# A hybrid decoder layer on one core: three activation blocks requested ahead of the big weight quarters, and the last root applied as a factor per partition

## The chip, the cores and the metric

The kernel runs on one core of one Trainium2 chip. The metric is the device time of one execution in microseconds (us), lower is better. Rows of the profile call the engines PE (TensorE), DVE (VectorE), ACT (ScalarE), POOL (GpSimd) and SP (SyncE, which here issues every transfer between memory and the on-chip buffers).

## The reference

One layer over 1024 tokens of width 1024, all in float32:

```
mod = silu(c) @ w_ada + b_ada            # nine rows: shift, scale, gate, three times
u = rmsnorm(h, ffn1_norm)*(1+sc1)+sh1;   h = h + 0.5*gt1*swiglu(u, ffn1_w_in, ffn1_w_out)
u = rmsnorm(h, mix_norm)*(1+sc2)+sh2;    h = h + gt2*token_mixer(u)
u = rmsnorm(h, ffn2_norm)*(1+sc3)+sh3;   h = h + 0.5*gt3*swiglu(u, ffn2_w_in, ffn2_w_out)
out = rmsnorm(h, final_norm)             # x * rsqrt(mean(x*x) + eps) * gain
swiglu(x, w_in, w_out) = (silu(g) * v) @ w_out,  g, v = split(x @ w_in)     # hidden width 2816
```

The token mixer (gated linear attention and differential attention) is not touched by the change.

## The kernel before

The activations `h` are kept transposed: 128 channels on the partitions, 8 channel tiles `k`, 1024 tokens along the row. Tokens are worked in two halves of 512. Each float32 operand of a product is split into a high part and a low part, and a product is three matmuls (high by high, high by low, low by high). ScalarE makes the high part, GpSimd the low part of a weight and VectorE the low part of an activation.

**The down projection of each FFN** (`down(f)`, f = 0 and 1) is done with seven products of half-size blocks in place of eight. Each product goes over the 11 pairs of hidden tiles, so there are 77 steps `n` of 12 matmuls (line 2428). A step needs one activation block, 128x512, from `hid_dram`: the hidden activations are written to memory block by block (`hidden_out`, 256 KB each) and read back (`hidden_in(f, n)`, 256 KB) into four buffers `x_raw`, by turns. ScalarE copies block n to its high part (`x_highs`, line 1251), VectorE subtracts for the low part (`x_low`, line 1818, which counts up `x_ready`). `hidden_in(f, n)` with n >= 4 waits until `x_ready` says that block n - 4 has been split. `x_op`, the split operand, has three buffers, so ScalarE can take block n when step n - 3 has been done.

The weights come in four quarters, Q00, Q10, Q01 and Q11, each 11 blocks of 256 KB. Q00 comes in parts: loads 6 and 0 (2 and 6 blocks), 1 (2 blocks) and 2 (the last block); loads 3, 4 and 5 are Q10, Q01 and Q11 whole, 2816 KB each. Products 0, 1 and 6 use Q00, Q01 and Q11 as they are; the others use sums (`weight_sum`, half of them on GpSimd, half on VectorE): Q00 - Q10 from step 4 on, then Q11 less that, from step 15 on, and so on. ScalarE makes the high part of the weight of step n + 3 in its turn n, right behind the activation block n (`high_hs`), so from turn 8 on it needs Q01.

SyncE issues all loads and stores in one written order, and waits where that order says so. The waits on `hs_used` are for products of the last hidden tile, whose operands lie where the quarters go. The wait on `hid_out` is for all stores of activations, before the first block that the last hidden tile has written is read (product 1 on).

**The tail.** Product 6 gives the channel tiles 4 to 7 of the second token half, into the banks `ps[4]` to `ps[7]`. VectorE adds them to `h` (`reads(1, 6)`, line 1873), ScalarE squares them (line 1152), VectorE adds the squares up over the channel tiles (line 1726), TensorE sums over the partitions with a matrix of ones (`mean_square`, line 2261), ScalarE takes the root (lines 1157 and 1160), VectorE multiplies `h` by gain and root (`final_y`, line 1731), TensorE transposes 128x128 pieces (line 2807), four to a bank, ScalarE copies each bank into `o_tile` (line 1617), and SyncE stores one tile of 128 tokens by 1024 channels (512 KB) at a time. The first token half has its root and its scaling during the last steps of the down projection; its transposes come right behind the last step.

## Time and profile before

| | |
|---|---|
| median of 3 runs | 2260.81 us (2259.23 to 2266.37) |
| the profiled execution | 2263.8 us, span 2262.1 us from the first to the last instruction |
| mean granted TensorE clock | 0.987 of full speed |
| TensorE busy | 2181.8 us, 96% of the span |
| VectorE, ScalarE, GpSimd busy | 1266.0, 817.0, 1286.4 us |
| moved by DMA | 236.27 MB, 104 GB/s over the span |

The span is what the profile covers; the execution's own time is 1.7 us more. Shares are of the span. The granted clock is 1.00 at 2.4 GHz and 0.50 at 1.2 GHz. The down projection of the first FFN runs from about 501 to 710 us, that of the second from 2017 to 2237 us.

### The profile page before, as it was taken

The numbers are of one execution on the slowest core, as the hardware profiler recorded it, in microseconds if no ns is written. First come the engines' busy times: TensorE is split into PE (matmuls) and PEld (weight loads), VectorE is DVE, ScalarE is ACT, GpSimd is POOL, SyncE is SP. The second block draws the span as 40 slices with busy tenths as digits, with TensorE's granted clock in tenths as the row PEclk, the third lists the DMA queues.
The fourth block names the chain that finished last, engine by engine and source line by source line (L and its number), as shares of the span: only waits on it lengthen the run. The fifth ranks groups of instructions, "written<-read, shape, count | busy, mean of one in ns | idle before, by whom it ended". The sixth has DMA issues, their size and how long they took to land.

```text
span 2262.1 us, 27922 instructions
## 1 busy us (share of the span) xinstructions
PE 2181.8 (96%) x10289; PEld 1761.5 (78%) x10289; DVE 1266.0 (56%) x1971; ACT 817.0 (36%) x1513; POOL 1286.4 (57%) x1036
## 2 busy tenths in 40 slices
PE   7999999998999999999999999999999999999997
PEld 4688888886887777778777788888778888878886
DVE  6956666667857327656655202243955444458845
ACT  5522232233445314355545201023523333233444
POOL 5677878878854432312212233336778887768841
PEclk9999999999999999999999999999999999999999
DMA  9054454566333310011101113111053333364332
GB/s 345 28 168 154 152 159 139 169 233 215 94 102 113 103 47 1 11 29 38 29 28 31 45 47 121 47 47 47 24 174 115 112 98 112 98 257 147 99 98 103
DMA packets 222793, 236.27 MB, mean 104 GB/s; under 512 B 9775, under 2 KB 154306, under 8 KB 222402
## 3 DMA queue, kind: packets, MB, share of 16 engines
q1 hardware_dynamic: 222658, 234.49, 31.9%
q8 instruction: 83, 1.36, 0.2%
q14 instruction: 52, 0.43, 0.1%
HBM read 185.69 MB, written 48.76 MB: 104 GB/s over the span
## 4 chain that ended last, share of the span: by engine, by line
PE 77%; DVE 8%; ACT 4%; DMA 3%; issue 3%; POOL 2%; SPq 1%; DVEq 0%; ACTq 0%; POOLq 0%
PE ps L2371 30%; PE ps L2428 15%; PE ps L2242 13%; PE ps L2325 12%; POOL w_lo L987 1%; DMA x_raw<-hid_dram 1%; DVE h L2038 1%; DMA ada_full<-in_w_ada 1%; PE ps L2513 1%; PE ps L2623 1%; PE ps L2287 1%; DVE x_op L1818 1%; ACT h L1485 1%; PE ps L2588 1%; DVE h L2061 1%
## 5 line engine op out<-in xcount | busy, mean ns | idle before, releaser
L2428 PE MATMUL ps<-x_op,w_hi 128*128 128x512 f32 x1232 | 385.0, 394 | 13.5 <-DVE x_op L1818 13.5
L2371 PE MATMUL ps<-t,w_hi 128*128 128x512 f32 x1280 | 395.5, 390 | 1.1 <-POOL w_lo L987 1.0
L987 POOL TENSOR_TENSOR w_lo<-w_raw,w_hi 128x512 fp32r<-128x512 f32 x240 | 347.4, 1460 | 63.1 <-ACT w_hi L1241 63.1
L952 POOL TENSOR_SCALAR w_hi<-w_raw 128x1024 fp32r<-128x1024 f32 x55 | 57.8, 1050 | 471.3 <-PE ps L2242 295.7
L1241 ACT ACTIVATE w_hi<-w_raw 128x512 fp32r<-128x512 f32 x240 | 143.8, 626 | 414.7 <-DMA w_raw<-in_ffn_w_in 172.7
L2428 PEld LDWEIGHTS ps<-x_op,w_hi 128*128 128x128 f32 x1232 | 233.5, 190 | 65.1 <-issue 14.5
L2371 PEld LDWEIGHTS ps<-t,w_hi 128*128 128x128 f32 x1280 | 239.4, 188 | 52.3 <-POOL w_lo L987 2.4
L987 POOL TENSOR_TENSOR w_lo<-q,w_hi 128x512 fp32r<-128x512 f32 x132 | 193.2, 1468 | 125.4 <-ACT w_hi L1241 125.4
L2371 PE MATMUL ps<-t,w_lo 128*128 128x512 f32 x640 | 249.1, 389 | 0.0
L2428 PE MATMUL ps<-x_op,w_lo 128*128 128x512 f32 x616 | 241.6, 392 | 0.0
L1818 DVE TENSOR_TENSOR x_op<-x_raw,x_op 128x512 fp32r<-128x512 f32 x154 | 161.8, 1062 | 120.4 <-ACT x_op L1251 119.8
L2371 PE MATMUL ps<-b_low,w_hi 128*128 128x512 f32 x640 | 197.3, 389 | 0.9 <-POOL w_lo L987 0.9
L1251 ACT ACTIVATE x_op<-x_raw 128x512 fp32r<-128x512 f32 x154 | 97.3, 632 | 238.4 <-PE ps L2428 205.3
L958 POOL TENSOR_TENSOR w_lo<-w_raw,w_hi 128x512 fp32r<-128x512 f32 x128 | 178.1, 1411 | 7.0 <-ACT w_hi L1283 1.8
L1648 DVE SCALAR_TENSOR_TENSOR ada_acc<-ada_half,c_act,ada_acc 128x512 f32<-128x512 f32 x84 | 95.2, 1134 | 141.4 <-DMA ada_half<-in_w_ada 141.4
L2242 PE MATMUL ps<-u_hi,w_hi 128*128 128x512 f32 x368 | 150.6, 409 | 0.0
L2242 PE MATMUL ps<-u_lo,w_hi 128*128 128x512 f32 x368 | 145.0, 394 | 0.0
L2242 PE MATMUL ps<-u_hi,w_lo 128*128 128x512 f32 x368 | 144.7, 393 | 0.0
L2371 PEld LDWEIGHTS ps<-b_low,w_hi 128*128 128x128 f32 x640 | 119.9, 188 | 26.6 <-issue 1.8
L2371 PEld LDWEIGHTS ps<-t,w_lo 128*128 128x128 f32 x640 | 120.1, 188 | 25.3
L2428 PEld LDWEIGHTS ps<-x_op,w_lo 128*128 128x128 f32 x616 | 116.9, 190 | 24.8
L2371 PE MATMUL ps<-b_low,w_lo 128*128 128x512 f32 x320 | 124.5, 389 | 0.0
(292 smaller groups left out, 4271.8 us busy)
## 6 DMA issues: line engine op xcount, KB each, us to landing
w_raw<-in_ffn_w_in SPq DMA_DIRECT2D x88, 512.0 KB, 4.4
hid_dram<-hid_raw SPq DMA_DIRECT2D x154, 256.0 KB, 5.2
x_raw<-hid_dram SPq DMA_DIRECT2D x154, 256.0 KB, 2.6
ada_half<-in_w_ada SPq DMA_DIRECT2D x96, 256.0 KB, 3.2
w_raw<-in_w_in SPq DMA_DIRECT2D x41, 512.0 KB, 3.6
q<-in_ffn_w_out SPq DMA_DIRECT2D x6, 2816.0 KB, 12.2
ada_full<-in_w_ada SPq DMA_DIRECT2D x24, 512.0 KB, 11.4
x_tile<-in_x SPq DMA_DIRECT2D x8, 512.0 KB, 5.1
```

The source lines that it names most:

```text
L952: nc.gpsimd.tensor_scalar(w_hi[:, slot, :], w_raw[:, slot, :], 1.0, 0.0, ALU.mult, ALU.add).then_inc(w_high, 1)
L958: low_ = nc.gpsimd.tensor_tensor(w_lo[:, slot, half(c)], w_raw[:, slot, half(c)], w_hi[:, slot, half(c)].bitcast(F32), ALU.subtract)
L987: nc.gpsimd.tensor_tensor(lo, src, hi.bitcast(F32), ALU.subtract).then_inc(hs_ready, 1)
L1241: nc.scalar.activation(hs_place(n)[0], src, ACT.Copy).then_inc(wa_high, 1)
L1251: nc.scalar.activation(x_op[:, n % 3, 0, :], x_raw[:, n % 4, :], ACT.Copy).then_inc(x_high, 1)
L1485: nc.scalar.activation(x, x, ACT.Exp, bias=nmx[:, i % 2, m:m + 1], accum_out=lsum[:, i % 2, m:m + 1]).then_inc(exp_ready, 1)
L1648: nc.vector.scalar_tensor_tensor(acc, ada_half[:, c, :], c_act[:, k:k + 1], acc, ALU.mult, ALU.add).then_inc(half_used, 1)
L1818: nc.vector.tensor_tensor(x_op[:, n % 3, 1, :], x_raw[:, n % 4, :], x_op[:, n % 3, 0, :].bitcast(F32), ALU.subtract).then_inc(x_ready, 1)
L2242: mm = nc.tensor.matmul(out_, w[i], x[j], start=(start and q == 0), stop=(stop and q == 2))
L2325: mm = nc.tensor.matmul(ps[bank + hf][:], w[:, slot, c], u[:, hf, k, :], start=(k == 0 and u is u_hi and w is w_hi), stop=(k == KT - 1 and ...
L2371: mm = nc.tensor.matmul(ps[bank][:], w[i], x[:, k, :], start=(first and k == 0 and q == 0), stop=(k == 3 and q == 2), skip_group_check=True)
L2428: mm = nc.tensor.matmul(ps[down_bank(p) + m][:], w[:, tile(m)], x_op[:, n % 3, x, :], start=(p in (0, 1, 3) and k == 0 and q == 0), stop=( ...
```

## The change

Two parts. In `down(f)` on SyncE, the requests of activation blocks 4 to 6 move ahead of Q10; block 7 stays behind the last part of Q00, the stores of the last hidden tile and block 8 come next, then Q01, blocks 9 and 10, the wait for all stores, block 11, Q11, and the rest.

In the tail, the second token half is transposed without its root. Channel tiles 0 to 3 are multiplied by the gain during steps 44 to 47, in place; channel tiles 4 to 7 get it from the transposing matmul itself, whose right operand is a diagonal matrix of the gains (`gain_diag`, made in steps 60 to 63) in place of the identity. The mean square of the second half becomes four products with one column of ones, so that it comes out as a factor per token, with the tokens on the partitions (`rs_col`, 128x4). ScalarE applies it in its copy of the first half of each output row, VectorE in its copy of the second half. The stores of the last four tiles are made in halves of 256 KB, twelve stores in all.

```diff
@@ SyncE, down(f)
                 quarter_load(f, 1, q00[:, 0:2, :], 0, 0, 8, 10)
+                for i in range(4, 7):
+                    hidden_in(f, i)
                 sp.wait_ge(hs_used, n + 5)
                 quarter_load(f, 3, q10[:], 1, 0, 0, PAIRS)
                 sp.wait_ge(hs_used, n + 7)
                 quarter_load(f, 2, q00[:, 10:11, :], 0, 0, 10, 11)
-                quarter_load(f, 4, q01[:], 0, 1, 0, PAIRS)
-                for i in range(4, 8):
-                    hidden_in(f, i)
+                hidden_in(f, 7)
                 hidden_out(f, LAST)
                 hidden_in(f, 8)
+                quarter_load(f, 4, q01[:], 0, 1, 0, PAIRS)
+                for i in range(9, 11):
+                    hidden_in(f, i)
                 sp.wait_ge(hid_out, 16 * (f + 1) * DOWN_STEPS)
+                hidden_in(f, 11)
                 quarter_load(f, 5, q11[:], 1, 1, 0, PAIRS)
-                for i in range(9, DOWN_STEPS):
+                for i in range(12, DOWN_STEPS):
                     hidden_in(f, i)
@@ SyncE, stores
+                if t < 4:
+                    sp.wait_ge(o_ready, 4 + t + 1)
+                    sp.dma_start(out[0][t * P:(t + 1) * P, :], o_tile[t]).then_inc(o_stored, 16)
+                    continue
+                sp.wait_ge(o_ready, 4 + t + 1)
+                sp.dma_start(out[0][t * P:(t + 1) * P, half(0)], o_tile[t][:, half(0)]).then_inc(o_stored, 16)
+                sp.wait_ge(o_dve, t - 3)
+                sp.dma_start(out[0][t * P:(t + 1) * P, half(1)], o_tile[t][:, half(1)]).then_inc(o_stored, 16)
@@ ScalarE, tail
+            for i in range(8):
+                kg, t = i // 4, i % 4
+                if i in (2, 3):
+                    squares(3, 8 + 2 * i, 10 + 2 * i)
                 act.wait_ge(y_t, i + 1)
+                nc.scalar.activation(o_tile[t][:, half(kg)], ps[i][:], ACT.Copy).then_inc(o_ready, 1)
+            act.wait_ge(ms_done, 8)
+            nc.scalar.activation(rs_col[:], ps[7][:, 0:4], ACT.Ln, bias=eps_c[:, 0:1], scale=1.0 / D).then_inc(ln_ready, 1)
+            act.wait_ge(ln_ready, 8)
+            nc.scalar.activation(rs_col[:], rs_col[:], ACT.Exp, scale=-0.5).then_inc(rstd_ready, 1)
+            act.wait_ge(rstd_ready, 8)
+            for j in range(4):
+                act.wait_ge(y_t, 8 + j + 1)
+                nc.scalar.activation(o_tile[4 + j][:, half(0)], ps[j][:], ACT.Copy,
+                                     scale=rs_col[:, j:j + 1]).then_inc(o_ready, 1)
@@ VectorE, down(f) and tail
+                    if f == 1 and 44 <= n < 48:
+                        dve.wait_ge(sq_ready, sq_count(3, 1, n - 44))
+                        nc.vector.tensor_scalar(h[:, n - 44, half(1)], h[:, n - 44, half(1)], final_gain(n - 44), None,
+                                                ALU.mult).then_inc(y_ready, 1)
+                    if f == 1 and 60 <= n < 64:
+                        nc.vector.tensor_scalar(gain_diag[:, n - 60, :], ident[:], final_gain(4 + n - 60), None,
+                                                ALU.mult).then_inc(diag_ready, 1)
@@
-            for k in range(KT):
-                final_y(1, k)
+            for j in range(4):
+                dve.wait_ge(y_t, 12 + j + 1)
+                nc.vector.tensor_scalar(o_tile[4 + j][:, half(1)], ps[4 + j][:], rs_col[:, j:j + 1], None,
+                                        ALU.mult).then_inc(o_dve, 1)
@@ TensorE, tail
+            for i in range(12):
+                kg, t = i // 4 % 2, 4 * (i // 8) + i % 4
                 if i % 4 == 0:
+                    pe.wait_ge(y_ready, (8, 12, 4)[i // 4])
+                if i == 4:
+                    pe.wait_ge(acc_done, 2 * READS)
+                if i >= 8:
+                    pe.wait_ge(o_ready, i - 7)
                 for k in range(4 * kg, 4 * kg + 4):
+                    mm = nc.tensor.transpose(ps[i % 8][:, tile(k - 4 * kg)], h[:, k, tile(t)], ident[:])
+                mm.then_inc(y_t, 1)
+            pe.wait_ge(o_ready, 8)
+            pe.wait_ge(sq_used, half_added(3, 1))
+            for j in range(4):
+                mm = nc.tensor.matmul(ps[7][:, j:j + 1], rstd[3][1][:, tile(j)], ones[:, 0:1], start=True, stop=True)
+            mm.then_inc(ms_done, 1)
+            pe.wait_ge(diag_ready, 4)
+            for j in range(4):
+                if j == 3:
+                    pe.wait_ge(ln_ready, 8)
+                for k in range(4):
+                    mm = nc.tensor.matmul(ps[4 + j][:, tile(k)], h[:, 4 + k, tile(4 + j)], gain_diag[:, k, :], start=True,
+                                          stop=True)
                 mm.then_inc(y_t, 1)
```

## Rows read from the trace of the kernel before

**Rows 1.** The page: the span, and busy time, share and instructions of each engine.
```profile
span 2262.1 us, 27922 instructions
PE 2181.8 (96%) x10289; PEld 1761.5 (78%) x10289; DVE 1266.0 (56%) x1971; ACT 817.0 (36%) x1513; POOL 1286.4 (57%) x1036
```

**Rows 2.** Busy time by window: its length, each engine, clock, DMA share, GB/s.
```profile
2017.00:2237.40 220.40, 214.29 (x930) 175.87 (x929) 151.33 (x141) 94.65 (x164) 148.58 (x99) 0.98 0.40 130
2237.40:2262.10 24.70, 11.24 (x67) 9.19 (x65) 10.88 (x16) 11.86 (x22) 0.00 (x0) 0.78 0.42 170
```

**Rows 3.** Timeline of PE: start, us, instructions, [idle before <- releaser].
```profile
518.18 1.19 PE L2428 MATMUL ps<-x_op,w_hi 128*128 128x512 f32 x2 [6.36 <-DVE x_op L1818]
...
2033.59 1.19 PE L2428 MATMUL ps<-x_op,w_hi 128*128 128x512 f32 x2 [5.31 <-DVE x_op L1818]
```

**Rows 4.** Timeline of ACT in both down projections: copies of activation blocks.
```profile
523.73 0.63 ACT L1251 ACTIVATE x_op<-x_raw 128x512 fp32r<-128x512 f32 x1 [3.90 <-PE ps L2428]
...
2039.14 0.63 ACT L1251 ACTIVATE x_op<-x_raw 128x512 fp32r<-128x512 f32 x1 [3.90 <-PE ps L2428]
...
2042.16 0.63 ACT L1251 ACTIVATE x_op<-x_raw 128x512 fp32r<-128x512 f32 x1 [1.86 <-PE ps L2428]
...
2053.04 0.63 ACT L1251 ACTIVATE x_op<-x_raw 128x512 fp32r<-128x512 f32 x1 [1.56 <-PE ps L2428]
...
2055.76 0.63 ACT L1251 ACTIVATE x_op<-x_raw 128x512 fp32r<-128x512 f32 x1 [1.56 <-PE ps L2428]
```

**Rows 5.** The chain of waits, in order of time: start, us, what.
```profile
501.83 14.75 DMA x_raw<-hid_dram
...
2037.61 9.65 DMA x_raw<-hid_dram
```

**Rows 6.** Timeline of SP, second down projection: transfers issued.
```profile
2017.43 0.82 SPq L772 DMA_DIRECT2D q<-in_ffn_w_out  x2
2018.29 4.60 SPq L767 DMA_DIRECT2D x_raw<-hid_dram  x1
...
2025.84 2.75 SPq L761 DMA_DIRECT2D hid_dram<-hid_raw  x5
```

**Rows 7.** Busy time by window, columns as in rows 2.
```profile
2003.00:2032.00 29.00, 25.28 (x112) 20.61 (x110) 13.55 (x14) 9.07 (x14) 13.72 (x10) 1.00 1.02 384
```

**Rows 8.** Timeline of DVE: block 3 split, last hidden product.
```profile
2022.34 1.78 DVE L1818 TENSOR_TENSOR x_op<-x_raw,x_op 128x512 fp32r<-128x512 f32 x1
2024.04 1.77 DVE L1794 TENSOR_TENSOR hid_raw<-hid_raw 128x512 f32<-128x512 f32 x1
```

**Rows 9.** Timeline of DVE at block 46, then one group by line and form.
```profile
2149.45 0.68 DVE L1818 TENSOR_TENSOR x_op<-x_raw,x_op 128x512 fp32r<-128x512 f32 x1
...
L1644 DVE TENSOR_SCALAR ada_acc<-ada_half,c_act 128x512 f32<-128x512 f32 x12 | 9.1, 755 | 0.0
```

**Rows 10.** Timeline of DVE and of ACT right behind the last step.
```profile
2237.47 2.73 DVE L1873 SCALAR_TENSOR_TENSOR h<-ps,gate_c,h 128x512 f32<-128x512 f32 x4 [5.42 <-PE ps L2428]
...
2237.91 2.06 ACT L1617 ACTIVATE o_tile<-ps 128x512 f32<-128x512 f32 x4 [7.90 <-PE ps L2807]
```

**Rows 11.** Timeline of PE in the tail.
```profile
2244.07 1.90 PE L2261 MATMUL ps<-bufs,ones 128*128 128x512 f32 x2 [3.14 <-DVE bufs L1726]
2250.18 5.81 PE L2807 MATMUL ps<-ident,h 128*128 128x128 f32 x32 [4.21 <-DVE h L1731]
```

**Rows 12.** Groups by line and form: busy us, mean ns of one, idle before.
```profile
L2311 PE MATMUL ps<-ones,ada_acc 128*128 128x1 f32 x128 | 14.9, 246 | 2.2 <-DVE ada_acc L1632 2.2
L2574 PE MATMUL ps<-far,h 128*128 128x128 f32 x64 | 8.6, 278 | 0.0
```

**Rows 13.** Busy time by window in the tail, columns as in rows 2.
```profile
2244.00:2245.00 1.00, 0.93 (x2) 0.33 (x2) 0.02 (x1) 0.00 (x0) 0.00 (x0) 0.64 0.86 352
2254.00:2255.00 1.00, 1.00 (x9) 1.00 (x8) 0.00 (x0) 0.77 (x2) 0.00 (x0) 0.74 0.00 0
2256.00:2261.00 5.00, 0.00 (x0) 0.00 (x0) 0.00 (x0) 0.79 (x2) 0.00 (x0) 1.00 0.99 406
```

More of the change, by code:

```diff
@@ L102, in build_program @@
         heads2 = sb("heads2", [P, 2])
-        sb("pad", [P, 80])
+        rs_col = sb("rs_col", [P, 4])
+        sb("pad", [P, 76])
         h = sb("h", [P, KT, S])
@@ L155, in build_program @@
             s2_b = at(st_, "s2_b", [P, 4, HALF])
+        with stage() as st_:
+            at(st_, "pad_diag", [P, 64 * 1024 // 4])
+            gain_diag = at(st_, "gain_diag", [P, 4, P])
         with stage() as st_:
@@ L397, in build_program @@
         o_ready = sem("o_ready")
+        o_dve = sem("o_dve")
+        diag_ready = sem("diag_ready")
         o_stored = sem("o_stored")
@@ L898, in _ @@
             for t in range(TT):
-                sp.wait_ge(o_ready, 8 * (t // 4) + 4 + t % 4 + 1)
-                sp.dma_start(out[0][t * P:(t + 1) * P, :], o_tile[t]).then_inc(o_stored, 16)
-            sp.wait_ge(o_stored, 16 * TT)
+                if t < 4:
[6 more added lines that the diff above has]
+                sp.dma_start(out[0][t * P:(t + 1) * P, half(1)], o_tile[t][:, half(1)]).then_inc(o_stored, 16)
+            sp.wait_ge(o_stored, 16 * 12)
         @block.gpsimd
@@ L1608, in _ @@
             ffn(1)
-            for i in range(2 * TT):
-                hf, kg, t = i // 8, i // 4 % 2, 4 * (i // 8) + i % 4
-                if i == 4:
-                    squares(3, 12, 14)
-                if i == 6:
-                    squares(3, 14, 16)
-                    root(3, 1)
-                act.wait_ge(y_t, i + 1)
-                nc.scalar.activation(o_tile[t][:, half(kg)], ps[i % 4 + 4 * hf][:], ACT.Copy).then_inc(o_ready, 1)
+            for i in range(8):
+                kg, t = i // 4, i % 4
+                if i in (2, 3):
+                    squares(3, 8 + 2 * i, 10 + 2 * i)
+                act.wait_ge(y_t, i + 1)
+                nc.scalar.activation(o_tile[t][:, half(kg)], ps[i][:], ACT.Copy).then_inc(o_ready, 1)
[8 more added lines that the diff above has]
+                                     scale=rs_col[:, j:j + 1]).then_inc(o_ready, 1)
         @block.vector
@@ L1726, in adds, with final_gain, final_y @@
                     nc.vector.tensor_tensor(rstd[n][hf], rstd[n][hf], sq_b[n][c % 2], ALU.add).then_inc(sq_used, 1)
-            def final_y(hf, k):
-                g0 = ROWS["final_norm"][0] + k
-                nc.vector.scalar_tensor_tensor(h[:, k, half(hf)], h[:, k, half(hf)], vecT[:, g0:g0 + 1], rstd[3][hf],
+            def final_gain(k):
+                return vecT[:, ROWS["final_norm"][0] + k:ROWS["final_norm"][0] + k + 1]
+            def final_y(k):
+                nc.vector.scalar_tensor_tensor(h[:, k, half(0)], h[:, k, half(0)], final_gain(k), rstd[3][0],
                                                ALU.mult, ALU.mult).then_inc(y_ready, 1)
```

10 lines of the change are left out of this document (1 added, 9 removed).

## The prediction

> **What bounds the kernel now.** I read the page first: TensorE is busy for 96% of the span [rows 1], so only its idle time and its slow time can be won. Next, busy time by stage: the second FFN's down projection and the tail behind it [rows 2]. The down projection of each FFN is 77 steps of 12 matmuls; its steady pace is read from ScalarE, which is released once a step: 2055.76 - 2053.04 = 2.72 us [rows 4]. Two holes stand out in TensorE's timeline, one at step 4 of each down projection: 6.36 and 5.31 us [rows 3]. Behind each the clock is at half: ScalarE's releases put the end of step 4 at 523.73 and 2039.14, so step 4 took 5.55 us from its start in rows 3, and step 5 took 2042.16 - 2039.14 = 3.02 [rows 4]. The chain of waits then names the cause: block 4 of the hidden activations, asked for at 501.83 and landed 14.75 us later [rows 5]. The tail is 24.7 us in which TensorE works 11.2 [rows 2].
>
> Why block 4 is late is a sum of bytes. One SyncE queue carries everything. From 2003 to 2032 it moved 29 us x 384 GB/s = 11.1 MB [rows 7]. In front of and with blocks 4 to 6 stand: the last activation stores 0.52, blocks 0 to 3 1.05, the three small parts of quarter Q00 2.62, Q10 2.88, the last part of Q00 0.26, Q01 2.88, blocks 4 to 6 0.79: 11.0 MB. So the queue is served in order and is full. From 2018.29 SyncE even stood 4.60 us in the request of block 4 itself, with Q10, Q00's end and Q01 (6.0 MB) outstanding [rows 6].
>
> **The change, part 1: the order of the loads.** Each load keeps its size; only the order moves.
>
> What it removes. Blocks 4 to 6 now stand behind 0.52 + 1.05 + 2.62 + 0.79 = 5.0 MB. Counting back from 2032 at 0.41 MB/us, they land at 2032 - 6.0/0.41 = 2017.4. Step 4 is due where the hole now begins, 2033.59 - 5.31 = 2028.3, less some 0.2 us in which the last matmul drains: 2028.1. ScalarE can take block 4 two steps earlier, at 2022.7. The hole goes, in both FFNs: 6.36 + 5.31 = 11.7 us. With it goes the half clock: (5.55 - 2.72) + (3.02 - 2.72) = 3.1 us each, 6.2 for both. Together 17.9 us. TensorE is then never idle for long there, so nothing in the rows would lower its clock.
>
> What is late next. Q10 is 0.79 MB later: lands at 2024.3. GpSimd's first weight sum and, behind it in its queue, the low half of step 5's weight wait for it: 2024.3 + 1.5 + 1.5 = 2027.3, due one step after 2028.1, at 2030.8. Hidden, margin 3.5 us.
>
> Q01 is the next. Before, it was asked for at 2017.8 [rows 6]. Now SyncE first waits for block 3's low half (2024.12) for block 7, then for the last product (2025.82) [rows 8], issues five stores in 2.75 us [rows 6], then block 8: Q01 goes out at about 2029.3, some 11.5 us later. How long a quarter takes on a queue that has run empty: at the old Q11, the quarter went out at 2037.2 and block 9 behind it landed 9.65 us after 2037.61 [rows 5], 10.1 us for both, so 9.4 for a quarter. With 0.5 us of stores still ahead Q01 lands at 2039.2. Its first reader is ScalarE's copy for step 11, and queued behind that copy is activation block 9: 2039.2 + 0.6 + 0.6 + 0.7 (VectorE's low half) = 2041.1, due 2028.1 + 5 x 2.72 = 2041.7. It just fits.
>
> Q11, and block 12 behind it, are the tightest. By the 6.0 MB above, the request of Q11 (2.88, with Q01 2.88 and blocks 9 to 11 0.79 outstanding: 6.6) should be held until Q01 has landed, 2039.2; block 12 then lands 10.1 us later, at 2049.3, and is split at 2050.6, or at 2051.7 if VectorE's operation takes 1.78 us instead of 0.69, as in [rows 8] beside a busy GpSimd. Step 12 is due at 2028.1 + 8 x 2.72 = 2049.9. That is a new hole of 0.7 to 1.8 us; I take 1.5. In the first FFN the DMA never runs dry before Q01: it lands 1.8 MB behind the old landing at 516.6, at 521.1; block 12 lands at about 531.5, split by 532.8; step 12 is due at 518.18 - 6.36 - 0.1 + 8 x 2.72 = 533.5. I take 0.5. Cost of the new holes: 2.0 us; bounds 0 (all fits) and 12.4 (below). No request is added; SyncE issues three of 0.4 us ahead of Q10 (asked for at about 2012) while 4.2 - (11.0 - 20 x 0.41) = 1.4 MB are still queued: nothing.
>
> **Part 2: the tail.** Moved under the down projection: four gain multiplications of 128x512 on VectorE in steps 44 to 47. The nearest kind took 0.48 to 1.4 us, mean 0.76 [rows 9]. Two of them stand ahead of block 46's low half, which before ended at 2150.13 [rows 9]; step 46 is due 31 steps ahead of the end, at about 2152. Cover 1.9 us against 1.0 to 2.8: I take 0, bound 1 us. Four 128x128 multiplications in steps 60 to 63 are hidden.
>
> The new tail, on the old time axis, where the last down matmul ends at 2237.4 (VectorE is released by it at 2237.47 [rows 10]):
> - VectorE's last residuals end at 2240.20 as before [rows 10]; the four sums of squares follow at 0.7 each with ScalarE's squares between them, to 2243.2 (before they ended when the mean square could start, at 2244.07; two copies, not four, now stand ahead of the squares).
> - TensorE: 16 transposes to 2239.1, a wait of 1.1 us for the residuals, then 32 more, the last four of them behind ScalarE's fourth copy, to 2243.9.
> - ScalarE: eight copies at 2.06/4 = 0.51 us [rows 10] and four squares that wait for the sums, to 2245.0. That frees the last bank; TensorE waits 1.1 us for it.
> - Mean square as four 1-column products: 8 instructions of 14.9/128 = 0.12 us [rows 12]: to 2246.0. Before, one 512-column product took 1.90 us, mostly at half clock, and ended at 2245.97 [rows 11, 13].
> - Root on 128x4: 0.5 to 0.6 us, beside TensorE, which no longer waits for it. The eight 0.68 us scalings and the 4.21 us hole ahead of the second transposes [rows 11] are gone.
> - In their place 16 products with the gain's diagonal, two instructions each. Nearest row: the same shape, 8.6/64 = 0.134 us an instruction at full clock [rows 12]: 32 x 0.134 = 4.3, to 2250.4. VectorE's last scaled read 0.75: 2251.2.
> - The output. Before, the last four tiles (2.1 MB) moved from 2256.1 to 2261.2 at 406 GB/s [rows 13], and the span ended 0.9 us later. Now all 4.2 MB are asked for from 2243.4 on and faster than the queue moves them: start 2244.2, 4.2/0.41 = 10.2 us, end 2254.4, span end 2255.3. So the queue, and not the engines (2251.2 + some 3 us for 256 KB), ends the tail.
>
> Gain 2262.1 - 2255.3 = 6.8 us.
>
> Whether TensorE's clock stays full there: it fell at 2244.36 (the window 2244 to 2245 has 0.64) after 3.1 us of idle time [rows 11, 13]; the new waits are 1.1 us each. If it fell, 32 instructions at twice 0.134 are 8.6 us and the small products 1.9: compute ends at 2256.4, the span at 2259: gain 3.1. The Trainium skill ("TensorE: Matmul & The Clock Gate", Part 4: PE-mode transpose) says that transposes do not count as work for the clock; by it the long run of transposes would leave the tail at half, the 3.1 us case. The trace speaks against it: the clock came back inside the second set of transposes, with nothing else on TensorE since 2250.18 (0.74 in 2254 to 2255) [rows 11, 13]. I take full.
>
> **Sum.** 17.9 - 2.0 + 6.8 = 22.7 us. The profiled execution took 2263.8: 2241.1. It stands 3.0 above the median of the three runs; on that median, 2260.8 - 22.7 = 2238.1.
>
> **Rivals.**
> - *The hole moves to step 9 or 12 and takes the clock with it.* It needs Q01 or block 12 some 2 us later than worked out, for instance because stores and reads share the queue at less than 0.41 MB/us. Price: 3.1 us idle, the least in these rows after which the clock fell, and 3.1 us at half clock, in both FFNs: 12.4 instead of 2.0. Time 2248.5. For it: my margins are 0.6 us and negative. Chance 0.17.
> - *The tail at half clock.* 2260.8 - 15.9 - 3.1 = 2241.8. Chance 0.15.
> - *The tail gives nothing* (the output queue gets half-rows through more slowly, or the chain of squares is longer): 2260.8 - 15.9 = 2244.9. Chance 0.05.
> - *The loads don't do what the order says* (block 4 early, but an equal hole later): tail alone, 2254. Chance 0.04.
> - *Slower.* One mechanism: Q01 goes out after block 8, which itself waits for a split block, and ScalarE stands in order behind Q01. It decides once the new hole passes 17.9 + 6.8 = 24.7 us in all, 12.4 in each FFN, so once Q01 lands after 2039.2 + 0.6 + 12.4 = 2052. At 15 us each: 2266. Against it: SyncE's waits ahead of Q01 are all for work that rows 8 place before 2026. Chance 0.03.
> - My forecast: 0.56.
>
> **Numbers.** Differences under 0.3% (6.8 us) can't be told from no change here. Faster: my forecast, the first three rivals, and half of the fourth: 0.56 + 0.17 + 0.15 + 0.05 + 0.02 = 0.95; I say 0.94; same 0.03; slower 0.03. Range 2233 to 2249: below, no new hole (2236) less the scatter of the runs; above, the moved hole.
>
> **What would show it.** Right: no wait of ScalarE for an activation block at step 4; TensorE's clock 1.00 through both down projections; a short wait at step 12, longer in the second FFN; in the tail a clock of 1.00, TensorE done at about 13 us after the last down matmul, and the output queue busy without a break for the last 10 us. Wrong: a hole of over 3 us at step 9 or 12 with 0.50 behind it; clock 0.50 over the products with the diagonal; gaps in the output queue.

## The result and the profile after

The changed kernel takes 2251.72 us (median of 6 runs, 2247.95 to 2252.55); the kernel before took 2261.20 beside it (6 runs, 2259.23 to 2266.37). The ratio is 0.995, with a 95% interval of 0.994 to 0.9961: faster by 9.5 us between the medians, or 0.5%. The sign is as predicted, the size is not: 22.7 us were forecast, and 2251.72 lies above the range of 2233 to 2249.

The page of the kernel after, span and busy time of each engine, answers to [rows 1]; behind it busy time by window (length; TensorE, its weight loads, VectorE, ScalarE, GpSimd, each with its instructions; clock; DMA share; GB/s), which answers to [rows 2]:

```profile
span 2246.2 us, 27974 instructions
PE 2173.8 (97%) x10311; PEld 1755.1 (78%) x10311; DVE 1270.0 (57%) x1975; ACT 813.2 (36%) x1509; POOL 1289.1 (57%) x1036
```
```profile
500.80:711.00 210.20, 205.46 (x899) 168.01 (x898) 144.49 (x139) 96.68 (x169) 148.22 (x99) 1.00 0.47 149
2010.00:2230.00 220.00, 214.29 (x950) 175.57 (x949) 162.09 (x155) 97.36 (x170) 148.47 (x99) 1.00 0.41 130
```

The clock is 1.00 through both down projections. The two holes of [rows 3] are gone. What stands in their place, in the timeline of TensorE (start, us, instructions, idle time before and its releaser):

```profile
515.76 0.73 PE L2462 MATMUL ps<-x_op,w_hi 128*128 128x512 f32 x2 [1.27 <-POOL w_lo L1003]
...
2036.13 0.70 PE L2462 MATMUL ps<-x_op,w_hi 128*128 128x512 f32 x2 [1.77 <-DVE x_op L1843]
2039.53 0.70 PE L2462 MATMUL ps<-x_op,w_hi 128*128 128x512 f32 x2 [0.40 <-DVE x_op L1843]
2049.28 0.70 PE L2462 MATMUL ps<-x_op,w_hi 128*128 128x512 f32 x2 [1.22 <-DVE x_op L1843]
```

These are step 5 of the first FFN and steps 9, 10 and 13 of the second, whose step 0 now begins 7.5 us earlier than before (first product with the low half of the weight at 2010.17 instead of 2017.69). Many small waits have taken the place of two long ones. To count them all I took, from the same timeline, the time from one step's first `w_lo` matmul to the next step's, and what it has over 2.72 us:

```
us over 2.72 a step     FFN 1: where                              sum   FFN 2: where                               sum
before                  4 and 5: 9.3; 13 .9; 14 .7; 72 .9         11.8  4 and 5: 8.3; 13 .7; 14 .7; 72 .9          10.6
after                   5 1.6; 9 1.0; 10 .7; 12 .9; 13 1.5;        7.2  9 2.0; 10 .7; 12 .1; 13 1.5; 14 .7;         6.9
                        14 .7; 72 .9                                    47 1.0; 72 .9
```

The sums are those before rounding. Of every kernel that ran I also cut the profiled span at the first and the last start of a down matmul on `w_hi` (head, down 1, middle, down 2, tail):

```
kernel (profiled execution)        head   down 1  middle   down 2  tail    span    GB/s in 498 to 514
before                             500.8  220.8   1295.7   219.6   25.3    2262.1  409
before, second profile (e1)        501.5  222.3   1292.5   219.8   24.9    2260.9  409
after                              500.7  216.2   1292.8   215.9   20.6    2246.2  390
after, second profile (e4)         501.5  216.1   1295.2   215.8   20.8    2249.4  389
e2 order of the loads alone        500.6  214.4   1295.8   213.9   24.2    2248.9  404
e3 tail alone                      501.9  223.6   1295.2   223.4   20.4    2264.5  390
e5 whole rows stored               502.1  217.0   1298.9   216.0   19.7    2253.6  389
e6 halves stored, nothing else     500.0  223.1   1292.5   221.5   25.4    2262.5  409
e7 new buffers declared, unused    501.6  223.2   1294.9   220.8   25.1    2265.6  389
e8 gain 4 steps later              501.9  215.9   1294.0   214.6   20.7    2247.0  390
e9 after, buffers back in line     501.8  215.5   1292.4   215.1   20.6    2245.3  407
e10 before, buffers 32 bytes off   503.0  223.4   1296.3   221.4   24.2    2268.2  390
e11 e9 and Q01 ahead of block 8    500.8  215.2   1291.4   215.9   20.7    2244.0  399
e12 combined                       500.0  213.4   1293.1   212.5   20.4    2239.4  398
e13 e12 and first halves early     500.1  213.6   1292.8   213.8   17.7    2238.0  394
e14 e12 and Q01 in two parts       501.3  212.5   1293.9   212.1   20.1    2240.0  408
e15 both                           499.7  212.1   1295.2   212.1   17.7    2236.8  377
```

Two profiles of one kernel differ by 3.2 us in the middle and by 1.5 us in the first down projection, and e6, which orders its loads as the kernel before does, has 2.3 and 1.9 us more than before in its two down projections. So a cause is read from rows inside a stage, or from several timed runs, and not from one span. The last column depends on the order of the loads too (e12 to e15); for the rate of the queue, compare kernels with the same order. In the first pair the down projections gave 4.6 + 3.7 = 8.3 us and the tail 4.7: 13.0 against 22.7.

The end, timelines of TensorE, ScalarE, VectorE and SyncE's queue:

```profile
2226.10 1.91 PE L2841 MATMUL ps<-ident,h 128*128 128x128 f32 x16
...
2229.17 3.69 PE L2841 MATMUL ps<-ident,h 128*128 128x128 f32 x32 [1.16 <-DVE h L1898]
2233.64 1.05 PE L2846 MATMUL ps<-ones,bufs 128*128 128x1 f32 x8 [0.78 <-ACT o_tile L1630]
2234.55 3.82 PE L2853 MATMUL ps<-gain_diag,h 128*128 128x128 f32 x32
```
```profile
2235.26 2.42 ACT L1638 ACTIVATE o_tile<-ps,rs_col 128x512 f32<-128x512 f32 x4
```
```profile
2235.80 3.36 DVE L2267 TENSOR_SCALAR o_tile<-ps,rs_col 128x512 f32<-128x512 f32 x4 [3.78 <-PE ps L2853]
```
```profile
2232.15 3.68 SPq L911 DMA_DIRECT2D out_h<-o_tile  x4
```

and its windows, columns as above:

```profile
2229.00:2238.00 9.00, 8.05 (x71) 7.84 (x72) 4.69 (x8) 6.94 (x14) 0.00 (x0) 1.00 0.54 211
2233.00:2244.00 11.00, 4.73 (x40) 4.54 (x40) 3.01 (x4) 3.48 (x8) 0.00 (x0) 0.98 0.98 379
2244.00:2245.00 1.00, 0.00 (x0) 0.00 (x0) 0.00 (x0) 0.00 (x0) 0.00 (x0) 0.50 0.07 27
```

The last down matmul ends at 2226.1. The engines are done at 2235.80 + 3.36 = 2239.2, 13.1 us later. The queue runs full from 2233 to 2244 (11 us x 379 GB/s = 4.2 MB). Behind that the DMA share is 0.07: one of the 16 DMA engines is still at work, and the trace has one packet in flight at any time until 2245.5. The span ends 0.8 us later.

### The profile page after: what moved, and what is told of

Read it like the earlier page. It is cut to its first block, busy times and chain, and to the rows that moved or that the text cites. A ratio compares the mean times of both kernels' runs of the same rounds, so it can differ in the third digit from the quotient of the medians.

```text
span 2246.2 us, 27974 instructions
## 1 busy us (share of the span) xinstructions
PE 2173.8 (97%) x10311; PEld 1755.1 (78%) x10311; DVE 1270.0 (57%) x1975; ACT 813.2 (36%) x1509; POOL 1289.1 (57%) x1036
## 4 chain that ended last, share of the span: by engine, by line
PE 75%; DVE 9%; ACT 4%; DMA 4%; issue 3%; POOL 3%; SPq 1%; DVEq 0%; ACTq 0%; POOLq 0%
PE ps L2405 30%; PE ps L2462 14%; PE ps L2276 13%; PE ps L2359 12%; DMA x_raw<-hid_dram 1%; POOL w_lo L1003 1%; DVE x_op L1843 1%; DVE h L2070 1%; DMA ada_full<-in_w_ada 1%; PE ps L2547 1%; PE ps L2657 1%; ACT h L1501 1%; PE ps L2321 1%; DMA q<-in_ffn_w_out 1%; PE ps L2622 1%
```

## The experiments

Each ratio is to the kernel before on the same chip, with its 95% interval. Kernels 1 to 4, 5 to 8, 9 to 12 and 13 to 15 each shared a chip; the kernel before had medians of 2261.36, 2260.78, 2261.91 and 2262.44 us there.

**e1, e2, e3, e4: each part alone.** e1 is the kernel before again, e4 the changed kernel again. e2 has the order of the loads and the old tail:

```diff
+                for i in range(4, 7):
+                    hidden_in(f, i)
                 sp.wait_ge(hs_used, n + 5)
                 quarter_load(f, 3, q10[:], 1, 0, 0, PAIRS)
...
                 hidden_in(f, 8)
+                quarter_load(f, 4, q01[:], 0, 1, 0, PAIRS)
```

e3 has the new tail, with its buffers and its gain steps, and the old order:

```diff
                 quarter_load(f, 2, q00[:, 10:11, :], 0, 0, 10, 11)
+                quarter_load(f, 4, q01[:], 0, 1, 0, PAIRS)
+                for i in range(4, 8):
+                    hidden_in(f, i)
-                hidden_in(f, 7)
```

> The kernel before once more, for its profile on the same chip as the next three. My ledger took the saturated queue at 408 GB/s from the old profile; the profile after shows 389. Theory 1 (the rate belongs to the chip or the run): here, too, the windows in front of the first hole show one rate, the same as in the next runs. Theory 2 (the new order itself slows the queue): about 408 here and 389 with the new order on the same chip.

> Only the new order of the loads, with the old tail. By the step tables of the two profiles the down projections lost 11.8 and 10.6 us before and 7.2 and 6.9 after, of which 1.0 is VectorE's gain multiplications; so about 9.3 us faster. By my forecast (17.9 - 2.0) it would be 15.9. If the rest of the program gives time back or takes it, the ratio says so and the step tables don't.

> Only the new tail, with the old order of the loads. By the two profiles 4.7 us in the tail less 1.0 us at step 47: 3.7 faster. By my forecast 6.8. The rival that the middle of the program changes for a reason of its own would show as a ratio that the stage lengths at both ends don't add up to.

> The changed kernel again, on this chip. If the parts add, its gain is e2 plus e3, 13.0 us by the profiles; the first measurement gave 9.5 between medians. If 13 is right, the 9.5 was another chip or the scatter of the stages between; if 9.5 comes again, something in the stages between takes 3.5 us back.

Measured: e1 2262.59 (one run); e2 2247.72, 0.9941 (0.9927 to 0.9955); e3 2265.26, 1.0015 (1.0006 to 1.0024); e4 2251.09, 0.9953 (0.9939 to 0.9968). The loads alone give 13.6 us; the tail alone costs 3.9, although its own stage is 4.5 us shorter (24.9 to 20.4). The two add up to 9.7, and both together gave 10.3. So the tail's part loses some 8 us outside the tail. The stage table gives a hint: in e3 both down projections are longer than in e1 (but the first is hardly longer than that of e6), and the queue moves less from 498 to 514 us: 390 GB/s, against 409 in before, e1 and e6 alike. The same window of e1, e3 and e2:

```profile
498.00:514.00 16.00, 14.49 (x64) 11.66 (x63) 8.74 (x10) 5.90 (x10) 11.79 (x9) 1.00 1.05 409
```
```profile
498.00:514.00 16.00, 14.90 (x66) 12.01 (x64) 7.59 (x10) 6.53 (x10) 9.68 (x8) 1.00 1.04 390
```
```profile
498.00:514.00 16.00, 16.00 (x72) 13.26 (x71) 13.19 (x14) 9.36 (x15) 9.96 (x7) 1.00 1.05 404
```

The DMA engines are as busy in all three (share 1.04 to 1.05) and get less through in e3.

**e5, e6, e7, e8: which piece of the tail's part.** e5 is the changed kernel with the last four tiles stored whole:

```diff
                 sp.wait_ge(o_ready, 4 + t + 1)
-                sp.dma_start(out[0][t * P:(t + 1) * P, half(0)], o_tile[t][:, half(0)]).then_inc(o_stored, 16)
                 sp.wait_ge(o_dve, t - 3)
-                sp.dma_start(out[0][t * P:(t + 1) * P, half(1)], o_tile[t][:, half(1)]).then_inc(o_stored, 16)
+                sp.dma_start(out[0][t * P:(t + 1) * P, :], o_tile[t]).then_inc(o_stored, 16)
```

e6 is the kernel before with its last four tiles stored in halves, nothing else:

```diff
-                sp.dma_start(out[0][t * P:(t + 1) * P, :], o_tile[t]).then_inc(o_stored, 16)
+                if t < 4:
+                    sp.dma_start(out[0][t * P:(t + 1) * P, :], o_tile[t]).then_inc(o_stored, 16)
+                    continue
+                for c in range(2):
+                    sp.dma_start(out[0][t * P:(t + 1) * P, half(c)], o_tile[t][:, half(c)]).then_inc(o_stored, 16)
```

e7 is the kernel before with the new buffers and semaphores declared and nowhere used:

```diff
+        rs_col = sb("rs_col", [P, 4])
-        sb("pad", [P, 80])
+        sb("pad", [P, 76])
+            gain_diag = at(st_, "gain_diag", [P, 4, P])
```

e8 is the changed kernel with the gain multiplications four steps later:

```diff
-                    if f == 1 and 44 <= n < 48:
-                        dve.wait_ge(sq_ready, sq_count(3, 1, n - 44))
+                    if f == 1 and 48 <= n < 52:
+                        dve.wait_ge(sq_ready, sq_count(3, 1, n - 48))
```

> The changed kernel with the last four tiles stored whole again, each behind both of its waits. Every profile with the new tail so far shows the queue at 389 to 390 GB/s in 498 to 514 us and about 410 in 16 to 34 us, every one with the old tail 404 to 409 and about 420, although the tail is over 2,200 us away. Theory 1 (it comes with the half-row stores, or with what they do to the program): about 409 and 420 here, the holes at steps 5, 9 and 12 shrink, and the kernel is 2 to 4 us faster than the changed one. Theory 2 (it comes with something else of the new tail): 390 stays, and only the tail changes, by the 2.3 us that the last store is issued behind VectorE's last read at most.

> The kernel before with nothing changed but that the last four tiles are stored in halves, both halves at once. Theory 1: 390 and 410 GB/s in the same windows, and some 2 to 4 us slower than before. Theory 2: 409 and 420, and the same time as before within 1 us.

> The kernel before with the buffers and semaphores of the change declared and used by nothing. A rival cause of the slower queue is where things lie. If so: 390 and 410 GB/s here. If not: 409 and 420.

> The changed kernel with the four gain multiplications in steps 48 to 51 and not 44 to 47, behind the stretch in which VectorE reads product 3 and still makes weight sums. The step table gave step 47 1.0 us more than its 2.72. If VectorE's backlog is the cause, that 1.0 us goes and the rest of the second down projection stays at its lengths; if not, a hole of the same size stands elsewhere.

Measured: e5 2252.94, 0.9965 (0.9953 to 0.9978); e6 2261.46, 1.0003 (0.9994 to 1.0012); e7 2267.32 (one run); e8 2249.66, 0.9947 (0.9932 to 0.9963). Half stores cost nothing by themselves. Whole rows shorten the tail by 0.9 us (20.6 to 19.7) and show no gain in the time. e8 takes away the 1 us of step 47 (down 2 from 215.9 to 214.6), which is too little for its time to be told from that of after. The surprise is e7: no instruction of it differs from before, and its queue is at 389 GB/s. It has new places of the buffers, and more declared semaphores.

**e9, e10, e11, e12: the place of the buffers, and Q01.** The diff has two lines that the section on the change doesn't show:

```diff
-        sb("pad", [P, 80])
+        rs_col = sb("rs_col", [P, 4])
+        sb("pad", [P, 76])
```

The 16 bytes of `rs_col` on each partition are taken off `pad`, so that what follows should stay in place. But in the compiled program `rs_col` takes 32 bytes. `h` begins at byte 9248 of each partition instead of 9216 = 36 x 256, and it and all buffers behind it, which most transfers read or fill, are 32 bytes off a multiple of 256. e9 is the changed kernel with the right pad:

```diff
-        sb("pad", [P, 76])
+        sb("pad", [P, 72])
```

e10 is the kernel before with a wrong one:

```diff
-        sb("pad", [P, 80])
+        sb("pad", [P, 88])
```

e11 is e9 with Q01 ahead of block 8 and the last stores:

```diff
                 hidden_in(f, 7)
-                hidden_out(f, LAST)
-                hidden_in(f, 8)
                 quarter_load(f, 4, q01[:], 0, 1, 0, PAIRS)
+                hidden_in(f, 8)
+                hidden_out(f, LAST)
```

e12 is e11 with blocks 11 to 13 ahead of Q11, the gain steps of e8 and the whole rows of e5:

```diff
-                hidden_in(f, 11)
+                for i in range(11, 14):
+                    hidden_in(f, i)
                 quarter_load(f, 5, q11[:], 1, 1, 0, PAIRS)
```

> The changed kernel with one number changed: the unused pad behind the new 16-byte buffer is 72 and not 76 elements long. The buffer takes 32 bytes of each partition, so with 76 every buffer behind it, h, the weights and the quarters, starts at 9248 and up instead of 9216, 32 bytes off a multiple of 256; with 72 they start where they did before. Theory 1 (the 32 bytes slow every transfer into and out of these buffers): 419 GB/s in 16 to 34 us and 404 to 409 in 498 to 514, down projections of 214.4 and 214.9 us instead of 216.1 and 215.8, tail 20.0, and about 17 us faster than before (13.6 of the loads alone, 4.5 of the tail, less 1.0 at step 47). Theory 2 (the slow rate comes with the new semaphores): 410 and 389 stay, and about 10 us.

> The kernel before with the unused pad 8 elements longer: the same buffers 32 bytes further on, no new name. Theory 1: 410 and 389 GB/s and 3 to 5 us slower than before, spread over the stages that wait for transfers. Theory 2: 419 and 409, no change.

> As e9, and Q01 is asked for right behind block 7, ahead of block 8 and the five stores. In the profile after, ScalarE waited 6.5 us for Q01 in front of step 9, and steps 9 and 10 took 2.7 us too long in the second FFN, 1.7 in the first. If Q01's request behind the stores is the cause, both go, and the time falls by 2 to 4 us below e9's. Rival: the bytes in front of Q11 are what counts, and the hole moves on to steps 12 to 14.

> As e11, and Q11 behind block 13, the gain multiplications in steps 48 to 51, and the last four tiles stored whole. Step 47's 1.0 us goes (e8), the tail is 1 us shorter (e5), and the holes at steps 12 to 14 shrink to the 1.4 us that the kernel before has there: 4 to 6 us below e9, some 22 us faster than before. Rival: GpSimd stands at the first sum with Q11, in turn 15, and step 16 or 17 gets a hole of its own.

Measured: e9 2246.21, 0.9931 (0.9918 to 0.9943); e10 2269.95, 1.0035 (1.0022 to 1.0047); e11 2246.76, 0.9937 (0.9923 to 0.9951); e12 2241.09, 0.9911 (0.9897 to 0.9926). Busy time by window of e10, then of e9:

```profile
16.00:34.00 18.00, 17.79 (x65) 9.66 (x64) 13.21 (x12) 13.11 (x25) 0.23 (x1) 1.00 1.03 409
498.00:514.00 16.00, 16.00 (x71) 12.95 (x69) 8.28 (x11) 7.34 (x12) 8.55 (x7) 1.00 1.05 390
```
```profile
16.00:34.00 18.00, 17.30 (x65) 9.43 (x64) 13.98 (x12) 13.71 (x26) 0.19 (x1) 1.00 1.03 420
498.00:514.00 16.00, 16.00 (x72) 13.27 (x71) 11.03 (x14) 9.88 (x16) 8.86 (x6) 1.00 1.05 407
```

This is a switch that works in both directions: the shift alone slows the queue from 419 to 409 and from 409 to 390 GB/s, and the kernel before by 8.0 us; the right pad gives the rates back, and some 4.9 us. The first window moves rows of 4 KB, the second rows of 2 KB; over 16 engines both losses are some 3.8 ns more for each row (an estimate from the four rates), so by these two windows the price is per row and not per byte. No shift but 32 bytes was run, so which boundary counts (64, 128 or 256 bytes) is not shown. The Trainium skill ("DMA: Bandwidth & Descriptors", section "How a descriptor splits into AXI transactions") says that a descriptor that doesn't begin at a multiple of 256 bytes begins its first transaction at the boundary below. By it a row of 2 KB in this case would take nine transactions instead of eight, and 65 beats of 32 bytes instead of 64: an estimate of 1.6% to 12.5% more, worked out from that page. The loss measured here is 4.6% (409 to 390), so the trace agrees in the direction, and the page gives no figure for it. The page speaks of what a transaction reads, and most transfers of this window write the shifted buffers, so it is the nearest rule and not a cause that is shown.

e11 had the same time as e9. ScalarE's timeline of e11 shows why:

```profile
2026.32 0.63 ACT L1267 ACTIVATE x_op<-x_raw 128x512 fp32r<-128x512 f32 x1 [3.89 <-DMA x_raw<-hid_dram]
...
2030.16 0.63 ACT L1267 ACTIVATE x_op<-x_raw 128x512 fp32r<-128x512 f32 x1 [2.69 <-DMA x_raw<-hid_dram]
...
2041.34 0.63 ACT L1267 ACTIVATE x_op<-x_raw 128x512 fp32r<-128x512 f32 x1 [7.88 <-DMA x_raw<-hid_dram]
```

Where ScalarE waited for Q01 in after, it now waits for the activation blocks behind Q01. ScalarE needs both in turn, so swapping them only renames the wait: the lost steps sum to 6.1 and 6.9 us, against 6.4 and 6.0 in e9. In the second FFN the loss moved on, as the rival had it: steps 9 and 10 lose 0.8 us instead of 1.1, step 12 loses 2.1 instead of 0.9. e12 has 4.4 and 3.5 (without the 1.0 us of step 47, as e8), and takes 5 to 6 us less than e9 and e11. The losses at step 12 (2.1 us in the second FFN of e11) are gone: a hole goes when the block that is due next stands ahead of a quarter that isn't due yet (here blocks 12 and 13 ahead of Q11).

**e13, e14, e15: the output's start, and Q01 in parts.** e13 is e12 with the first halves of the first four output tiles stored as soon as they are copied, their second halves later:

```diff
             ffn(1)
+            for t in range(4):
+                sp.wait_ge(o_ready, t + 1)
+                sp.dma_start(out[0][t * P:(t + 1) * P, half(0)], o_tile[t][:, half(0)]).then_inc(o_stored, 16)
```

e14 is e12 with Q01 in two parts, and block 8, the stores and block 9 between them; e15 is both:

```diff
-                quarter_load(f, 4, q01[:], 0, 1, 0, PAIRS)
+                sp.dma_start(q01[:, 0:4, :], rows[1][:, 0:4, 0:HALF]).then_inc(q01_first, 16)
                 hidden_in(f, 8)
                 hidden_out(f, LAST)
-                for i in range(9, 11):
-                    hidden_in(f, i)
+                hidden_in(f, 9)
+                quarter_load(f, 4, q01[:, 4:PAIRS, :], 0, 1, 4, PAIRS)
+                hidden_in(f, 10)
```

> As e12, and the first halves of output tiles 0 to 3 are stored as soon as ScalarE has copied them, from about 1.5 us behind the last down matmul on, the second halves where the whole tiles were. In e9, e12 and the profile after, the output queue moves its 4.2 MB without a break from 6 us behind that matmul on and the tail is 20.5 us whatever the size of the stores. Theory 1 (the tail is bound by the queue and by when its first store can go): 1 MB moves in time that was empty, the tail falls by 1.5 to 2.6 us. Theory 2 (it is bound by the engines' chain or by the fixed time behind the last store): no change within 0.5 us, or slower by the four stores more.

> As e12, and Q01 comes in two parts: blocks 0 to 3 (1 MB) where the whole of it stood, the other seven behind activation block 9. In e12 step 8 to 10 still lose 2.6 us in the first FFN and 0.7 in the second, with ScalarE waiting for an activation block behind Q01. If what counts is the number of bytes that stand between a block and its turn, steps 8 to 10 lose under 0.8 us in both, and the time falls by 1 to 2.5 us. Rival: GpSimd, which is behind with the low halves, holds step 9, and nothing changes.

> e13 and e14 together: the sum of the two differences, some 3 to 5 us below e12 if both theories 1 hold.

Measured: e13 2240.29, 0.9902 (0.9888 to 0.9917); e14 2241.24, 0.9907 (0.9892 to 0.9922); e15 2238.42, 0.9891 (0.9875 to 0.9908). SyncE's queue in the tail of e12 and of e13:

```profile
2225.45 3.37 SPq L912 DMA_DIRECT2D out_h<-o_tile  x4
2229.93 3.30 SPq L916 DMA_DIRECT2D out_h<-o_tile  x4
```
```profile
2221.99 4.64 SPq L911 DMA_DIRECT2D out_h<-o_tile  x4
2226.78 2.86 SPq L915 DMA_DIRECT2D out_h<-o_tile  x4
2231.26 2.93 SPq L919 DMA_DIRECT2D out_h<-o_tile  x4
```

The tail begins at 2218.9 in e12 and at 2220.3 in e13 (span less tail, in the table). From there the first store goes out after 1.7 us instead of 6.5, 4.8 us earlier, and the tail is 2.7 us shorter (20.4 to 17.7). Now the queue is not full any more, and it works to the end with all of its engines, with none that trails: 277 GB/s and a share of 0.70 over the window, and still 0.56 over the last 2 us.

```profile
2222.00:2237.00 15.00, 9.06 (x78) 8.42 (x76) 7.33 (x11) 8.57 (x17) 0.00 (x0) 0.98 0.70 277
2236.00:2238.00 2.00, 0.00 (x0) 0.00 (x0) 0.00 (x0) 0.00 (x0) 0.00 (x0) 0.58 0.56 229
```

In e12 one engine alone works on for 2.2 us behind the others (its window is in the last section). In e13 that is gone, and it is most of the 2.7 us; the other fifteen engines end only some 0.5 us earlier.

On one chip, the split of Q01 brought e13's 2240.29 to 2238.42, and the early halves e14's 2241.24 to 2238.42; the intervals of all three overlap. Against the kernel before on the same chip, e12 gained 20.8 us, e13 22.2, e14 21.2 and e15 24.0, so e14's forecast of 1 to 2.5 us below e12 is not borne out by its time. In the stages the split takes away most of the loss at steps 8 to 10 (2.6 us in the first FFN of e12, none in that of e14), and e14 lost 1.3 us anew at steps 35 and 36. There VectorE splits block 35 in 1.78 us beside a GpSimd that never pauses, against 0.68 in e12, where it does. e15 is the fastest kernel of the study, 24.0 us under the kernel before and some 13 under the changed one (measured on other chips).

## Why the prediction was wrong in size

**The removal, 17.9 us: right.** The old hole and the half clock behind it held 9.3 and 8.3 us, 17.6 in all, and both are gone from both FFNs. The reason given, bytes ahead of block 4 in a queue served in order, was right.

**"Each load keeps its size; only the order moves": the first step that failed.** The forecast took the queue's 0.41 MB/us of before for the kernel after. It was 0.39 (390 GB/s from 498 to 514), because the tail's new buffer shifts every buffer behind it by 32 bytes. The diff showed this buffer and the pad, and I read them as a change of nothing. Price: 4.9 us by e9 against e4 (2251.09; the ratios are 0.9953 and 0.9931). The two ran on different chips and their intervals just overlap (0.9939 and 0.9943), so the size is uncertain by some 4 us, and the two down projections show 1.5 us of it (216.2 + 215.9 against 215.5 + 215.1). That the shift costs time at all rests on e10, which ran beside the kernel before. How it shows in the second FFN, ScalarE's timeline of after:

```profile
2033.46 0.63 ACT L1257 ACTIVATE w_hi<-q 128x512 fp32r<-128x512 f32 x1 [6.53 <-DMA q<-in_ffn_w_out]
2034.08 0.63 ACT L1267 ACTIVATE x_op<-x_raw 128x512 fp32r<-128x512 f32 x1
...
2043.55 0.63 ACT L1267 ACTIVATE x_op<-x_raw 128x512 fp32r<-128x512 f32 x1 [6.24 <-DMA x_raw<-hid_dram]
```

Q01 was forecast for 2039.2 and block 12 for 2049.3 on the old axis, which is 2031.7 and 2041.8 on this one. They came at 2033.4 and 2043.5, each 1.7 us late. In e9, with the rate given back, ScalarE does not wait for Q01 there any more; its wait there ends with TensorE, and block 12 comes at 2042.09:

```profile
2031.62 0.63 ACT L1257 ACTIVATE w_hi<-q 128x512 fp32r<-128x512 f32 x1 [4.76 <-PE ps L2462]
...
2042.09 0.63 ACT L1267 ACTIVATE x_op<-x_raw 128x512 fp32r<-128x512 f32 x1 [6.55 <-DMA x_raw<-hid_dram]
```

**The new holes, forecast 2.0 us: mis-sized, and the largest part of the miss.** Against before, e9 lost 6.4 - 2.4 and 6.0 - 2.2 us in its down projections, where 2.4 and 2.2 are the losses at steps 13, 14 and 72 that before had as well: 7.8 us together, and after 4.8 + 4.7 = 9.5. e2, with no shift and no gain steps, lost 5.5. The term of 0.5 for the first FFN and 1.5 for the second, put at step 12 alone, missed two things.

The first is bytes. In the first FFN Q01 was forecast for 521.1, "1.8 MB behind the old landing". ScalarE's timeline of after, then of e9:

```profile
525.56 0.63 ACT L1257 ACTIVATE w_hi<-q 128x512 fp32r<-128x512 f32 x1 [6.06 <-DMA q<-in_ffn_w_out]
```
```profile
525.82 0.63 ACT L1257 ACTIVATE w_hi<-q 128x512 fp32r<-128x512 f32 x1 [5.97 <-DMA q<-in_ffn_w_out]
```

It came 4.4 us late with the shift, and still 3.6 us late without it (e9's down projection begins 1.1 us later). What now stands ahead of Q01 and stood behind it before is blocks 4 to 8 and the five stores of the last hidden tile, ten transfers of 256 KB: 2.6 MB and not 1.8, which is 2.0 us at 0.41 MB/us. The other 1.6 us of e9 are those by which the first block of this down projection was asked for later than before (489.88 against 488.30 in after; the same in e9, less the 1.1); the last 0.8 of after are the lower rate. In e2, which began 0.4 us earlier than before and is not shifted, ScalarE had Q01 at 523.45.

The second is a queue of work. VectorE's timeline of after in the second FFN, behind the arrival of Q01:

```profile
2034.74 1.24 DVE L1843 TENSOR_TENSOR x_op<-x_raw,x_op 128x512 fp32r<-128x512 f32 x1 [5.50 <-ACT x_op L1267]
2035.91 1.77 DVE L641 TENSOR_TENSOR q<-q 128x512 f32<-128x512 f32 x1
2037.61 3.46 DVE L1843 TENSOR_TENSOR x_op<-x_raw,x_op 128x512 fp32r<-128x512 f32 x2
2040.99 1.78 DVE L641 TENSOR_TENSOR q<-q 128x512 f32<-128x512 f32 x1
2044.22 0.69 DVE L1843 TENSOR_TENSOR x_op<-x_raw,x_op 128x512 fp32r<-128x512 f32 x1 [1.45 <-ACT x_op L1267]
2044.83 2.72 DVE L1898 SCALAR_TENSOR_TENSOR h<-ps,gate_c,h 128x512 f32<-128x512 f32 x4
2047.46 1.68 DVE L1843 TENSOR_TENSOR x_op<-x_raw,x_op 128x512 fp32r<-128x512 f32 x1
```

Blocks 9 to 11 stand ready when ScalarE is set free, and VectorE works them off with two sums of weights in between, at 1.7 to 1.8 us each beside a busy GpSimd. The forecast charged block 9 alone, at 0.7. So after step 9, step 10 starts late too (at 2039.53, behind block 10's split, which ends at some 2039.3). Step 13 is late for another reason: between the splits of blocks 12 and 13 VectorE's order has the four residuals of product 0 (line 1898, 2.72 us). Block 12 came at 2043.5, step 12 was just in time for it, and block 13 was not split before 2049.1. The kernel before has these four residuals in the same place, with block 12 in hand earlier, and lost 0.7 to 0.9 us at step 13 instead of 1.5. That the backlog at steps 8 to 10 is born of the late Q01 is what e14 shows, where these losses go with an earlier first part. That the slow 1.7 us is what makes step 10 late, and the residuals step 13, is read from these rows; no run took either away.

**The hold of Q11's request: wrong, without effect on the time.** Q11 "should be held until Q01 has landed". SyncE's timeline of after:

```profile
2020.78 1.09 SPq L778 DMA_DIRECT2D q<-in_ffn_w_out  x1
...
2026.29 0.44 SPq L778 DMA_DIRECT2D q<-in_ffn_w_out  x1
```

Q01 went out at 2020.78 (forecast 2029.3, here 2021.8), and Q11 was taken in 0.44 us at 2026.29, with Q01 still to land at 2033.4. Block 12 came 10.1 us behind Q01 all the same, as forecast: the queue moved blocks 9 to 11, Q11 and block 12 in that time, 3.93 MB at 0.39 MB/us. The right number came out of the wrong sum. Why Q11 was not held: at 2026.29 some 7.1 us x 0.39 MB/us = 2.8 MB of Q01 and 0.8 of blocks 9 to 11 were still to move, 3.6 MB, where the forecast counted Q01 whole and Q11 itself, 6.6. The request behind Q11, that of block 12, was the one held:

```profile
2029.27 4.67 SPq L773 DMA_DIRECT2D x_raw<-hid_dram  x1
```

It went through at 2033.94, and Q11 landed some 9 us later: 3.4 MB were left.

**Q10, forecast 0: left out in the first FFN.** "Hidden, margin 3.5 us" was worked out for the second FFN alone, where it held. In the first, GpSimd's timeline of after:

```profile
512.23 1.80 POOL L641 TENSOR_TENSOR q<-q 128x512 f32<-128x512 f32 x1 [4.74 <-DMA q<-in_ffn_w_out]
```

The sum of weights ends at 514.0 and the low half of the weight follows it, for a step 5 that is due at 500.7 + 5 x 2.72 = 514.3: 1.6 us lost in after, 0.8 in e9, and none in e2.

**The gain multiplications, forecast 0, bound 1: the bound.** Step 47 begins 1.0 us late in after and not in e8.

**The tail, 6.8 us forecast, 4.7 in its stage.** All up to the queue's start came as worked out: the first store 6.0 us behind the last down matmul (2232.15 against 2226.1; forecast 2243.4 against 2237.4), TensorE at full clock, the engines done at 13.1 us (forecast 2251.2, 13.8). The queue then took 11.0 us instead of 10.2 for the 4.2 MB, and 2.2 us passed from there to the end of the span instead of 0.9: 0.8 + 1.3 = 2.1 us, the whole difference. The 1.3 us are the one DMA engine that trails the others. The same stage is 20.6 in e9, but not for the same reason:

```profile
2239.00:2242.00 3.00, 0.00 (x0) 0.00 (x0) 0.00 (x0) 0.00 (x0) 0.00 (x0) 1.00 1.03 398
2243.00:2244.50 1.50, 0.00 (x0) 0.00 (x0) 0.00 (x0) 0.00 (x0) 0.00 (x0) 0.50 0.07 26
```

With the right pad the queue is at 398 GB/s (379 from 2233 to 2244 in after), and fifteen engines are done at 17.7 us behind the last down matmul's start instead of 18.4. The sixteenth ends at 19.8 or 19.9 us in both and hides the gain. The forecast had no term for an engine that trails. Why one does, and which, is open.

**The clock.** The rival of a tail at half clock (0.15) did not come: it is 1.00 from 2229 to 2238, although TensorE had done nothing but transposes from 2226.10 to 2232.86. The rule of the Trainium skill that transposes do not count as work ("TensorE: Matmul & The Clock Gate", Part 4: PE-mode transpose) would have it fall; the trace goes against it here too. The rival of the moved hole (0.17) was half right: the hole moved to steps 9 to 13, each piece at most 2.0 us, and the clock did not fall.

**The sum put right.** 22.7, less 4.9 for the shifted buffers, less 5.8 for the new holes of e9 with step 47 (7.8 against 2.0), less 2.1 in the tail, is 9.9 us; measured were 9.5. That they meet so closely is luck: the 4.9 alone is uncertain by some 4 us. The shift cost the kernel before 8.0 us and gave only 4.9 back in the changed one. Where this difference lies is open: head and middle hold most of e10's loss (1.5 and 3.8 us against e1), and they scatter by as much between kernels that do not differ there.

## What to carry to other kernels

A buffer of a few bytes can slow every transfer behind it: before a diff is costed, compare where each large buffer begins, in the compiled program and not in the declared sizes. When a stall in an ordered queue is removed, look at what the next arrival sets free all at once, and cost that backlog on the engine that has to work it off, at the duration that it has beside its busy neighbours. Count every transfer that now goes ahead of a load, stores included, in every place where the order is used: here the first FFN's queue was full and the second's was not. Swapping two loads that one engine needs in turn renames its wait; it takes a split of the big one, or an earlier start, to shorten it.

## What the runs showed of the hardware

- The 32-byte shift: 409 to 389 or 390 GB/s in the first FFN's down projection, 419 to 409 from 16 to 34 us, with the DMA engines shown as fully busy either way (share 1.02 to 1.05). The kernel before lost 0.35% (0.22 to 0.47).
- A request of SyncE that took over 1.5 us went through when about 3.5 MB of what had been asked for before it was still to move. The 17 traces have 40 such requests around the two down projections; by their packets 3.0 to 3.9 MB were left at the end of each, 3.5 in the median. This fits block 4 in before (held for 4.60 us, [rows 6]) and block 12 in after (4.67 us, 3.4 MB left), and Q11 in after, which met 3.6 MB and took 0.44 us; no request of up to 0.5 us met more than 4.1 MB. The size of the request itself does not seem to count: Q11 is 2.9 MB. Whether the limit is in bytes or in rows is open, since nearly all rows here are of 2 KB.
- At the end of the program one of the 16 DMA engines worked on alone for 1.5 us in after, 2.2 us in e9 and in e12, with the share at 0.04 to 0.08 (one engine is 0.06). In before, e13 and e15, where the queue had a pause during the tail, none did. From the last packet to the end of the span it was 0.7 to 0.8 us in every kernel. It is not the half stores: e12 stores whole rows, and this is its end:

```profile
2237.00:2239.40 2.40, 0.00 (x0) 0.00 (x0) 0.00 (x0) 0.00 (x0) 0.00 (x0) 0.50 0.04 17
```
